# Memory attention with product tiles between its units, in a two-block transformer kernel on one core

## What is computed

```
kv = rms_norm(mem, mem_gain) @ w_kv
km = rms_norm(kv[..., :512].reshape(B, M, 4, 128), k_gain)
vm = kv[..., 512:].reshape(B, M, 4, 128)
qm = rms_norm(q_cols.reshape(B, S, 4, 128), q_gain)
s  = einsum('bshd,bmhd->bhsm', qm, km) * 128 ** -0.5
o  = einsum('bhsm,bmhd->bshd', softmax(s), vm)
x  = x + (concat(mix, o) * silu(gate)) @ w_out
```

## Time and profile before

| what | us |
|---|---|
| median of 3 runs (2166.09 to 2173.65) | 2169.78 |
| profiled execution | 2169.27 |
| its span, first to last instruction | 2167.4 |
| PE busy | 2017.9 (93%) |
| DVE busy | 1178.5 (54%) |
| ACT busy | 1041.6 (48%) |
| POOL busy | 242.6 (11%) |
| DMA | 255.6 MB, mean 118 GB/s |

### The profile page before, as it was taken

The page is one execution under the profiler, slowest core; times in us unless marked ns, Lnnn a source line. Parts: engine busy times, 40 slices in busy tenths (PEclk is TensorE's granted clock), DMA queues, the critical chain, the costliest instruction groups (busy, mean ns, idle before and its releaser), DMA issues.

```text
span 2167.4 us, 28080 instructions
## 1 busy us (share of the span) xinstructions
PE 2017.9 (93%) x10551; PEld 1705.2 (79%) x10551; DVE 1178.5 (54%) x2428; ACT 1041.6 (48%) x1704; POOL 242.6 (11%) x345
## 2 busy tenths in 40 slices
PE   7999999999899998899999999999998899998988
PEld 7977666677777775698988898888777787877876
DVE  3344377444899997554444444533443535736752
ACT  4644434344788786644444344444433554344431
POOL 0611132010010000211122012201000000000000
PEclk9999999999999999999999999999999999999999
DMA  4411221136899998322222222222243312112120
GB/s 141 133 48 40 61 76 49 40 127 217 268 376 354 369 355 299 97 77 75 66 66 66 66 67 66 67 77 87 69 129 118 106 55 78 30 49 78 49 88 39
DMA packets 178018, 255.60 MB, mean 118 GB/s; under 512 B 13565, under 2 KB 92234, under 8 KB 177882
## 3 DMA queue, kind: packets, MB, share of 16 engines
q1 hardware_dynamic: 168832, 221.33, 31.5%
q0 software_dynamic: 8784, 31.92, 4.0%
q10 hardware_dynamic: 266, 0.52, 0.1%
HBM read 239.57 MB, written 14.16 MB: 117 GB/s over the span
## 4 chain that ended last, share of the span: by engine, by line
PE 76%; DVE 11%; ACT 7%; DMA 4%; issue 2%; ACTq 0%; SPq 0%; POOL 0%; DVEq 0%; POOLq 0%
PE pb L2277 51%; PE pb L2305 5%; DVE wlo L1488 4%; PE pb L2633 4%; ACT whi L906 3%; PE pb L2841 2%; PE pb L2656 2%; PE pb L2773 2%; DMA wraw<-w_down 2%; PE pb L2764 2%; PE pb L2357 2%; PE pb L2370 1%; DMA wraw<-w_up 1%; PE pb L2850 1%; PE pb L2520 1%
## 5 line engine op out<-in xcount | busy, mean ns | idle before, releaser
L1488 DVE TENSOR_TENSOR wlo<-wraw,whi 128x1024 fp32r<-128x1024 f32 (+4 forms) x430 | 489.6, 1150 | 573.9 <-ACT whi L906 570.5
L2277 PE MATMUL pb<-whi,AT_hi 128*128 128x512 f32 (+4 forms) x1992 | 767.4, 385 | 22.6 <-ACT arena L928 3.5
L2277 PE MATMUL pb<-whi,AT_lo 128*128 128x512 f32 (+4 forms) x1992 | 730.4, 367 | 0.0
L2277 PE MATMUL pb<-wlo,AT_hi 128*128 128x512 f32 (+4 forms) x1992 | 728.9, 366 | 0.0
L906 ACT ACTIVATE whi<-wraw 128x1024 fp32r<-128x1024 f32 (+4 forms) x446 | 440.3, 993 | 457.8 <-PE pb L2277 390.1
L2277 PEld LDWEIGHTS pb<-whi,AT_hi 128*128 128x128 f32 x1992 | 378.9, 190 | 99.1 <-issue 42.5
L2277 PEld LDWEIGHTS pb<-whi,AT_lo 128*128 128x128 f32 x1992 | 378.0, 190 | 45.9
L2277 PEld LDWEIGHTS pb<-wlo,AT_hi 128*128 128x128 f32 x1992 | 379.5, 191 | 39.3 <-issue 2.6
L2305 PE MATMUL pb<-arena 128*128 128x128 f32 (+1 forms) x1180 | 188.3, 287 | 49.1 <-ACT arena L941 15.5
L2305 PEld LDWEIGHTS pb<-arena 128*128 128x128 f32 (+1 forms) x1180 | 147.7, 149 | 89.6 <-ACT arena L941 23.2
L2633 PE MATMUL pb<-whi,AT_hi 128*128 128x512 f32 x256 | 104.2, 407 | 4.4 <-DVE wlo L1488 2.4
(11 more groups left out here) (309 smaller groups left out, 2336.3 us busy)
## 6 DMA issues: line engine op xcount, KB each, us to landing
wraw<-w_in_a SPq DMA_DIRECT2D x288, 128.0 KB
wraw<-w_gate SPq DMA_DIRECT2D x128, 256.0 KB
wraw<-w_up SPq DMA_DIRECT2D x128, 256.0 KB
wraw<-w_down SPq DMA_DIRECT2D x58, 512.0 KB
wraw<-w_in_b SPq DMA_DIRECT2D x40, 512.0 KB
wraw<-w_in SPq DMA_DIRECT2D x28, 512.0 KB
wraw<-w_mem_kv SPq DMA_DIRECT2D x16, 512.0 KB
wraw<-w_in_a SPq DMA_DIRECT2D x16, 512.0 KB
```

Of the source, the lines that this page charges most:

```text
L1488: dve.tensor_tensor(w_slot(wlo, p, p % SPL), raw_slot(p), w_slot(whi, p, p % SPL).bitcast(F32), ALU.subtract).then_inc(lo_done[p % SPL], 1)
L2277: mm = pe.matmul(ACC[t][:, 0:n], a, b, start=kc == 0 and q == 0, stop=i == c["count"] - 1 and kk == per - 1 and q == 2)
```

## The change

- GpSimd waits for the last expert piece to be loaded before it reads the rows back into `x1`.
- At the end of the experts ScalarE makes six of the eight squares ahead of the row transposes' rounding and two behind the fourth; VectorE's last gain and its small norm operations move likewise, and the feeds of `qm0`'s first pieces move ahead.
- `memory_attention(l)` runs two pieces of the next chunk (`qd0` or `fl0`, in `NEXT`) between the keys' and the queries' transposes, and `attention_beside` with the tiles of its other two pieces at every second unit (`BESIDE_MEM`). ScalarE's copies of the query transposes move behind its squares. `attention` goes; `attention_beside` learns the form without a mask.
- Behind the barriers the projections, feeds and flows of `qd0` and `fl0` go.
- In the output stage the gated rows' transposes stand between the tiles of `fin00`, and the memory transposes between tiles of `fin01`.

The diff, cut; the hunks stand in the order of the file: GpSimd, ScalarE (attention_beside, memory_stage, end of the experts, dilated heads, recurrence), then TensorE (attention_beside, memory_attention, dilated heads, output stage, recurrence). VectorE's feeds and flows change as ScalarE's.

```diff
         def outs(U):
-            return max(U - AU["mat0"], 0)
+            return U - AU["dil"]
...
+        NEXT = ("qd0", "fl0")
+        BESIDE_MEM = [[tiles_of(nm)[8 + i // 2] if i % 2 else None for i in range(16)] for nm in NEXT]
...
@@ -830,6 +832,7 @@
+            pool.wait_ge(*raw_loaded(piece_of["dn", NEXP - 1, 1]))
             for t in range(NT):
                 pool.dma_start(x1[:, t, :], x_moe[t * P:t * P + P, :]).then_inc(S(f"x_back{t}"), 16)
...
@@ -1001,9 +977,10 @@
-                        act.activation(s, s, ACT.Exp, bias=att_nm[:, U % 4:U % 4 + 1],
-                                       accum_out=att_l[:, U % 4:U % 4 + 1]).then_inc(att_p, 1)
+                        masked = u["mask"] is not None
+                        act.activation(s, s if masked else SC[U % 2][:, 0:u["kw"]], ACT.Exp, bias=att_nm[:, U % 4:U % 4 + 1],
+                                       scale=1.0 if masked else u["scale"], accum_out=att_l[:, U % 4:U % 4 + 1]).then_inc(att_p, 1)
...
@@ -1055,9 +1030,12 @@
-                head_norm(f"qm{l}", f"qm{l}", qm_tok, NT, ns[f"qm{l}"], msq,
-                          lambda h: tcopy(f"qm{l}", h, qmT[:, h, :], tb(f"qm{l}", h)))
-                attention(f"mat{l}", lambda i: mem_unit(l, i), 16)
+                head_norm(f"qm{l}", f"qm{l}", qm_tok, NT, ns[f"qm{l}"], msq)
+                for q in range(2):
+                    feed(chunks[CH[NEXT[l]]]["first"] + q + SPL)
+                for h in range(MH):
+                    tcopy(f"qm{l}", h, qmT[:, h, :], tb(f"qm{l}", h))
+                attention_beside(f"mat{l}", lambda i: mem_unit(l, i), 16, BESIDE_MEM[l])
...
@@ -1298,27 +1276,32 @@
+            for n in range(6):
+                square_of(n)
+            feed(chunks[j]["first"] + SPL)
             for k in range(KD):
                 hi("n2", k, AT_hi[:, k, :], tb("n2", k), g_n2[0][:, k:k + 1])
+                if k == 3:
+                    square_of(6)
+                    square_of(7)
+                    act.activation(sqrt_ready, ns["ffn"]["ms"][:, 0:1], ACT.Sqrt)
...
@@ -1359,7 +1342,8 @@
-                    feed(chunks[j]["first"] + q + SPL)
+                    if n or nm == "v":
+                        feed(chunks[j]["first"] + q + SPL)
...
@@ -1405,7 +1390,7 @@
-                evac(f"fl{hh}", lambda t: l_tok[:, t, :])
+                evac(f"fl{hh}", lambda t: l_tok[:, t, :], fed=hh == 0)
...
-                        pe.wait_ge(att_m, U - 1)
+                        pe.wait_ge(att_m if u["mask"] is not None else att_p, U - 1)
...
+                for q in range(2):
+                    project_piece(NEXT[l], q)
                 read_all(f"qm{l}")
...
-                attention(f"mat{l}", lambda i: mem_unit(l, i), 16)
+                if l == 0:
+                    pe.wait_ge(S("rs_perm"), 1)
+                attention_beside(f"mat{l}", lambda i: mem_unit(l, i), 16, BESIDE_MEM[l])
...
-                    project_piece(f"{'qkv'[i // 4]}d{hd}", i % 4)
+                    if hd or i >= 4:
+                        project_piece(f"{'qkv'[i // 4]}d{hd}", i % 4)
...
-            gated_t(0, 1)
-            gated_t(0, 2)
-            project("fin00", [TPU[f"y0{c}"] + k for c in range(3) for k in range(4)])
             for i in range(6):
-                if i == 4:
-                    memory_t(1)
-                project_piece("fin01", i)
+                ready(f"y0{i // 2}", (2 * i % 4, 2 * i % 4 + 1))
+                for t in range(NT):
+                    project_tile("fin00", i, t)
+                    if i < 2:
+                        gated_t(0, 1 + i, (t,))
+            for i in range(6):
+                for t in range(NT):
+                    project_tile("fin01", i, t)
+                    if i in (2, 3):
+                        memory_t(1, (NT * (i - 2) + t,))
...
-                project(f"fl{hh}")
+                if hh:
+                    project(f"fl{hh}")
```

## The result

| | before | after |
|---|---|---|
| median of the runs beside each other, us | 2166.09 (5 runs) | 2186.53 (2182.93 to 2188.13, 5 runs) |
| profiled execution (span), us | 2169.27 (2167.4) | 2186.59 (2184.8) |
| ratio to before | | 1.0084, 95% interval 1.0064 to 1.0105 |

The changed kernel is slower: by the ratio, which compares runs taken beside each other, about +18 us (+14 to +23), by the two profiled executions +17.3 (the medians above differ by 20.4). The forecast was +16.3 (2185.6 us).

What follows compares the result with a forecast made beforehand. TensorE, busy 93% of the span, was taken as the bound, time hanging on its gaps and lower clock. Terms -3.2+0+17.8-10.8+12.5 = +16.3 on 2169.27 gave 2185.6 us; range 2175 to 2197.

Steps and rivals of the forecast that it cites:

- C (4): Behind the first memory stage's barrier: TensorE stands 13.3 us, since kd0 needs qd0's banks, evacuated behind sine and cosine.
- E: Second memory stage: +12.5 us in all (10 to 16), including 8.9 us of idle TensorE behind its barrier.
- R1: Rival: waits behind both barriers don't come about; 2159.5 us, deciding if together under 6 us, not 22; chance 0.07.
- C (2): First memory attention loop: units without a tile wait 0.72 us each, plus first unit's latency 1.2; +2.8 us.
- C (1): Ahead of the first memory loop: two qd0 pieces, 8.4 us of work, lengthen the stretch by 6.1 us; -2.3.
- (3): Into the first memory stage's barrier: the last tile's piece is rounded and subtracted behind the last output; +1.7 us.
- (5): Clock behind the first memory stage's barrier: after the gap TensorE runs at 1.2 GHz for a while; +1.6 us (0 to 3.2).
- D: Output stage: transposes among fin00 and fin01 tiles lose their gaps and half clock; -10.8 us (-12.5 to -8).
- E (1): Ahead of the second memory stage's loop: the same gain as in the first stage, with 512 columns; -2.0 us.
- R4: Rival: lower clock lasts twice as long behind three long gaps and reaches the loops; +8, 2193.6 us; chance 0.08.
- A: End of experts: rows reloaded behind the last weights, which come 5.2 us earlier, closing TensorE's gaps; -3.2 us (-5.2 to +1).
- B: Row transposes after the experts: moved squares, gain and roots remove a 1.11 us gap but free accumulators no earlier; 0 (-1.1 to +1).

Runs made afterwards that it cites:

- early: After, with GpSimd issuing the transfers of tables, gains, positions and lower bounds ahead of the two barriers: 2173.89 us, ratio 1.0035 to before.
- early_order: `early`, plus ScalarE's sine and cosine behind qd0's squares and VectorE's angles behind its reductions: 2168.27 us, ratio 1.0005 to before.
- half: After, with the third and fourth pieces of qd0 and fl0 behind the barriers, no tile in the memory loops: 2177.08 us, ratio 1.0036 to before.
- mended: After, with early transfers, qd0's squares ahead of the sines, exponential ahead of copy-out, and the last two squares moved back: 2160.46 us, ratio 0.9963 to before.
- exp_first: After, with ScalarE doing the next unit's exponential ahead of the last unit's copy-out in both memory attentions: 2181.10 us, ratio 1.0053 to before.
- reload: Before, with only the four reloads of the rows made to wait for the last down weights: 2162.92 us, ratio 0.9978.
- cover: Before, with only the same early transfers as `early`: 2170.29 us, ratio 1.0011.
- squares_later: `reload_output` plus B, with its last two squares, table load and roots behind the accumulators' copies: 2149.72 us, ratio 0.9916 to before.
- tail: `reload` plus two squares, the last tile's gain and the roots moved among the row transposes: 2162.33 us, ratio 0.9979 to before.
- output: Before, with only the output stage's transposes put among the product tiles of fin00 and fin01: 2158.99 us, ratio 0.9960.
- mem: Before, with only the memory attention's new order (two pieces ahead of the loop, eight tiles in it): 2199.80 us, ratio 1.0149.
- reload_output: Before, with the delayed row reloads and the output stage's moved transposes only: 2152.12 us, ratio 0.9927.

## Why the prediction was right, step by step

**C (4) and E, the waits behind the barriers.** The term that decided was right in mechanism and size: 1.7+13.3 us forecast into and behind the first barrier, 14.5 more measured (GpSimd's first issue behind the barrier, at 933.93 before and 950.53 after, puts 1.8 of it ahead of the barrier and 12.8 behind); 2.2+8.9 forecast at the second, 11.8 measured. `early`, `early_order` and `half` show each of its parts: the transfers 6.8 us, the order on ScalarE and VectorE 4.1, and two pieces behind the barrier (8.4 us, with the last piece's rounding no longer ahead of it) that take 10.8 off it. One slip of addition: the forecast's own terms for the way into the first barrier, 0.99+1.15+0.3-0.49, make 1.95 and not 1.7.

**R1** said that the waits decide from a point: faster if together under 6 us. With 9.4 us left (`early_order`, 4.15 and 5.29) the kernel is level with before, so the side it names is right and the point was set too low by some 3 us.

**C (2), the loop.** Forecast +2.8, measured +5.2. The pitch was right: a pair of units takes 4.04 us, and the forecast's terms make 4.03 (two units of 1.13, a tile of 1.05, a wait of 0.72), though the wait in it is 0.57. What was sized too small is the start: from the first scores to the third unit's transposes it is 7.30 us (912.92 to 920.22), where the terms of two units and the 1.2 for the first unit's latency give 4.5; behind that the loop keeps the pair's pitch. The first transposes wait 1.02 there, and TensorE runs at the lower clock, which costs some 1.6 us by `mended` against `exp_first`. The loop before starts at the lower clock too (0.50 from 912 to 914), but its 21.5 us were measured with that, and the new loop's units were added up at full clock. That the copy ahead of the exponential is the cause of the 0.57 is shown by `exp_first`; the price of the earlier trace rows was right in kind.

**C (1), (3), (5) and D, E (1).** Ahead of the loops 6.03 us were forecast as 6.1. The clock behind the waits was +1.6 twice, with +0.7 for the pitch in C; measured +1.5 for both together in C and +2.3 in E. D was -10.8 and is -11.3 in after, -11.4 alone. R4, the lower clock twice as long, is out at the first barrier and half true at the second in this trace: 24 products take 2.4 us more than at full clock. Its other half, the loops at the lower clock, came about at the start of the first loop alone.

**A** was the right mechanism, sized too small: -3.2 forecast, -4.8 (-2.8 to -6.9) in the runs, and at the groups' last products -5.5 in `reload` (855.91 to 850.70, from a start at 822.57 where before had 822.25) and -4.3 in after. By the raw 6.3 us in after, and by the 5.5, the experts' end moved by more than the 5 us that the prediction had named as a sign of being wrong: the term was too small, though the sum hid it. The +1.5 that I gave back for ScalarE's two roundings ahead of the hidden values does not show: the groups behind keep their 2.67 and 1.71 us gaps. The Trainium skill (DMA: Bandwidth & Descriptors, Queues, rings and completion order) has each DMA engine go round-robin between the rows that have work, which was my +1 end. The landing times of the moved reloads, 6.4 to 11.8 us, are long enough for sharing, but nothing behind them came later.

**B** failed in one step: "the accumulators that its next chunk wants come free about as late as before" is exact (23.5 us in both), and the forecast stopped there. I had not asked what one gap of 2.65 instead of two of 1.1 and 1.35 does to the clock. It cost 1.5 us, more than the end of +1 that I had set.

That the sum came out 1.1 us from the profiled difference is in part luck: A's -3.1 and D's -0.5 stand against +1.5 of B, +1.0 of C and +2.2 of E, and 2.0 of A's lie ahead of the change.

## What to carry to other kernels

Before moving independent products to where they hide a small latency, ask what they hide where they stand: here the transfers and small operations behind the barrier, some 13 us, cost nothing for as long as four pieces of products stood beside them, and all of it afterwards. If they must go, issue the transfers ahead of the barrier and do first, on each engine, what frees the next banks. In the one-ahead loop here the order of exponential and copy-out on ScalarE decided whether TensorE waits at the units without a tile.

## What was not expected of the hardware

Whether a short gap costs the clock is not a matter of its length alone. At the queries' first product all eight kernels with a gap of 1.35 or 1.36 kept the full clock; all six with one of 2.64 to 2.66 fell to the lower level, and the twelfth product started 3.6 to 4.1 us after the first instead of 2.6. Some 28 us earlier every kernel has a gap of 2.67 or 2.68 ahead of the last down products. There eight kept the clock (the twelve products took 2.96 to 3.00 us: before, after, `reload`, `cover`, `early_order`, `half`, `squares_later`, `mended`) and six lost it (4.3 to 4.6 us: `tail`, `output`, `mem`, `early`, `reload_output`, `exp_first`), and the edits don't separate the two groups. The Trainium skill (TensorE: Matmul & The Clock Gate, Idle/cold and Busy/warm rows of Part 1) has the array fall to half rate when it idles; by these rows it does so at the same gap in one kernel and not in another, which is a cause of 1.5 us differences that no edit explains. A shorter gap can lose it as well: ahead of the first scores of the kernel before it is 2.26, behind a thin stretch, and the granted clock is 0.50 from 912 to 914. What else decides was not tried.

The cost of coming back did not follow the length of the wait. At the first barrier 72 products took 14.2 to 14.5 us behind some 15 us of idle time (after, `exp_first`, `mem`), 14.4 behind 8.2, 14.3 behind 4.1, and 15.0 behind the 4.2 of `half`, against 12.6 at full clock. At the second, 24 products took 7.9, 8.4 and 7.3 us behind nearly the same idle time (12.25 in after, 12.35 in `exp_first`, 12.33 in `mem`) and 7.8 to 8.0 behind 5.3, against 5.5. So shortening a wait saved its length and nothing of the clock.
